# Three rounds per pair of heads in a forgetting attention, with moved work at the head of the program and at a scan

## The reference

```python
def diff_attention(q, k, v, lam, lam_init, sub_g):     # 4 heads of 2 x 64, causal, 128-query blocks
    s = einsum('bqhmd,bkhmd->bhmqk', qi, kf) * scale + bias
    p = softmax(s); attn = p[:, :, 0] - lam * p[:, :, 1]
    o = einsum('bhqk,bkhe->bqhe', attn, vf)

def fox_mixer(q, k, v, f_raw, f_bias, q_norm_w, k_norm_w):   # 16 heads of 64
    cum = cumsum(log_sigmoid(f_raw + f_bias))
    for start in range(0, s, 128):                     # query blocks 0..3, keys 0..end
        end = start + 128
        logits = qh[start:end] @ kh[:end].T * scale + cum[start:end, None] - cum[None, :end]
        p = softmax(where(causal, logits, -inf))
        outs.append(p @ vh[:end])

x = x + concat([y_ssd, y_fox]) @ w_out                 # 2048 x 1024
x = x + (silu(gate) * val) @ w_down                    # after rms_norm, w_up, causal conv of 3 taps
```

## Time and profile before

| | us |
|---|---|
| median of 3 runs | 1915.64 |
| lowest, highest | 1915.46, 1917.94 |
| the profiled execution, whole | 1915.37 |
| its span, first to last instruction | 1913.5 |
| PE busy in the span | 1886.8 |
| DVE busy | 1181.0 |
| ACT busy | 790.7 |
| POOL busy | 140.0 |

### The profile page before, as it was taken

The page is one execution under the profiler, slowest core; times in us unless marked ns, Lnnn a source line. Parts: engine busy times, 40 slices in busy tenths (PEclk is TensorE's granted clock), DMA queues, the critical chain, the costliest instruction groups (busy, mean ns, idle before and its releaser), DMA issues.

```text
span 1913.5 us, 24463 instructions
## 1 busy us (share of the span) xinstructions
PE 1886.8 (99%) x9034; PEld 1504.5 (79%) x9034; DVE 1181.0 (62%) x1831; ACT 790.7 (41%) x1200; POOL 140.0 (7%) x102
## 2 busy tenths in 40 slices
PE   7999999999999999999999999999999999999999
PEld 6767888888887788888888887877666688888887
DVE  5686677356646866763576498565656566744762
ACT  4355444133435654441244433432466543422431
POOL 1011100000021110000000101111201020000000
PEclk9999999999999999999999999999999999999999
DMA  5211322322231122223222322344433123223222
GB/s 214 67 62 49 99 99 73 119 94 97 73 107 65 45 89 89 88 88 110 97 92 83 113 88 99 135 165 143 161 105 110 34 88 110 77 99 110 88 77 99
DMA packets 38304, 186.51 MB, mean 97 GB/s; under 512 B 4384, under 2 KB 4768, under 8 KB 23376
## 3 DMA queue, kind: packets, MB, share of 16 engines
q1 hardware_dynamic: 37936, 185.22, 28.5%
q10 hardware_dynamic: 288, 0.23, 0.0%
HBM read 176.95 MB, written 8.49 MB: 97 GB/s over the span
## 4 chain that ended last, share of the span: by engine, by line
PE 91%; DVE 5%; ACT 2%; issue 1%; DMA 0%; SPq 0%; POOL 0%; ACTq 0%; DVEq 0%; POOLq 0%
PE banks L709 55%; PE banks L1181 21%; PE banks L759 4%; DVE w_lo L1851 1%; PE banks L1120 1%; PE banks L1098 1%; DVE w_lo L2100 1%; PE banks L1107 1%; PE banks L1254 1%; PE banks L1225 1%; DVE tmp L2233 1%; PE banks L1070 1%; ACT w_hi L1334 1%; PE banks L1237 1%; PE banks L1194 1%
## 5 line engine op out<-in xcount | busy, mean ns | idle before, releaser
L709 PE MATMUL banks<-xn_hi,w_hi 128*128 128x512 f32 x1240 | 486.9, 393 | 10.5 <-DVE w_lo L2606 6.9
L709 PE MATMUL banks<-xn_hi,w_lo 128*128 128x512 f32 x1240 | 483.4, 390 | 0.0
L709 PE MATMUL banks<-xn_lo,w_hi 128*128 128x512 f32 x1240 | 478.2, 390 | 0.0
L1334 ACT ACTIVATE w_hi<-raw 128x2048 fp32r<-128x2048 f32 (+2 forms) x134 | 228.3, 1704 | 227.9 <-PE banks L709 192.3
L1851 DVE TENSOR_TENSOR w_lo<-raw,w_hi 128x2048 fp32r<-128x2048 f32 (+2 forms) x134 | 275.8, 2058 | 46.1 <-ACT w_hi L1334 45.7
L709 PEld LDWEIGHTS banks<-xn_hi,w_hi 128*128 128x128 f32 x1240 | 233.5, 188 | 62.3 <-DMA con<-consts 5.9
L709 PEld LDWEIGHTS banks<-xn_lo,w_hi 128*128 128x128 f32 x1240 | 233.5, 188 | 49.5 <-issue 1.4
L709 PEld LDWEIGHTS banks<-xn_hi,w_lo 128*128 128x128 f32 x1240 | 233.5, 188 | 48.8
L1396 ACT ACTIVATE tmp<-scaled_h,par 128x512 f32<-128x512 f32 x132 | 100.8, 809 | 349.8 <-DVE scaled_h L1896 349.7
L1896 DVE TENSOR_TENSOR scaled_h<-banks,token_rs 128x512 f32<-128x512 f32 x132 | 85.0, 686 | 186.3 <-PE banks L709 166.0
L1181 PE MATMUL banks<-xn_hi,w_hi 128*128 128x512 f32 x408 | 165.3, 405 | 1.0 <-DVE big L1946 0.6
(11 more groups left out here) (270 smaller groups left out, 2578.3 us busy)
## 6 DMA issues: line engine op xcount, KB each, us to landing
raw<-weights SPq DMA_DIRECT2D x116, 1024.0 KB, 4.9
raw<-weights SPq DMA_DIRECT2D x24, 768.0 KB, 4.3
raw<-weights SPq DMA_DIRECT2D x24, 640.0 KB, 3.9
big<-scratch SPq DMA_DIRECT2D x40, 256.0 KB, 4.8
att<-scratch SPq DMA_DIRECT2D x16, 256.0 KB, 4.7
scratch<-stage SPq DMA_DIRECT2D x12, 256.0 KB, 4.4
scratch<-con SPq DMA_DIRECT2D x12, 256.0 KB, 2.0
out<-x SPq DMA_DIRECT2D x4, 512.0 KB, 4.0
```

Of the source, the lines that this page charges most:

```text
L709: return pe.matmul(psum[:, 2 * p + m, :], w[:, at_:at_ + P], x_part(k), start=start, stop=stop)
L1334: act.activation(w_hi[:, sl], raw[:, sl], ACT.Identity).then_inc(hi_done, 1)
```

## The change

1. **Forgetting attention:** three rounds per pair in place of four. Blocks 0 and 1 share a round, side by side in the bank (columns 0 to 127 and 128 to 383), then block 2, then block 3. 26 steps in place of 34, with 12 products in each of 22 steps and 6 in each of the last four. ACT copies a pair's values at the first step of that pair, where it did so in the last step of the pair before. `x_scaled` stands ahead of the halves of `w_lo`, behind the bank reads.
2. **Scan:** products of steps 0 to 9 are 18, 20, 4, 4 and six times 3, in place of 18, 14 and eight times 4. `columns_taken` moves into `xbc`, between the taps of the last two chunks.
3. **Differential attention:** `w_lo` of the output slabs is made in two halves, in two successive steps.
4. **Head:** ACT rounds slab 1 behind the first square, and slab 2 ahead of `token_norm`; DVE subtracts slab 2 ahead of the first bank reads.

```diff
-S_PREP, S_POST, X_STEPS = 15, 4, 32
-S_FILL = weave([("S_Z", 4), ("X_IN", 12)], [18, 14] + [4] * 8 + [8] * 5 + shares(568, 2 * SSD_HEADS) + [24] * S_POST)
-X_FILL = weave([("S_OUT", 4), ("X_OUT", 2)], shares(192, 19) + shares(96, 15))
+S_PREP, S_POST = 15, 4
+X_ROUNDS = [(0, 1), (2,), (3,)]
+X_STEPS = 8 * len(X_ROUNDS)
+S_FILL = weave([("S_Z", 4), ("X_IN", 12)], [18, 20] + [4, 4] + [3] * 6 + [8] * 5 + shares(568, 2 * SSD_HEADS) + [24] * S_POST)
+X_FILL = weave([("S_OUT", 4), ("X_OUT", 2)], [12] * 22 + [6] * 4)
...
+        def f_blocks(r):
+
+            out, col = [], 0
+            for i in X_ROUNDS[r % 3]:
+                out.append((i, col, (i + 1) * P))
+                col += (i + 1) * P
+            return out
...
+                def mask(r):
+
+                    if r:
+                        pe.wait_ge(f_max, f_done(r))
                     for m in range(2):
+                        for i, col, w in f_blocks(r):
+                            pe.matmul(psum[:, 4 + m, col + i * P:col + (i + 1) * P], ident_b[:, :], mask_b[:, :],
+                                      start=(col == 0), stop=False, skip_group_check=True)
...
                     if it + 1 < X_PAIRS:
-                        if g % 4 < 2:
-                            x_norm_job(2 * (it + 1) + g % 4)
-                        elif g % 4 == 2:
+                        if g % 3 < 2:
+                            x_norm_job(2 * (it + 1) + g % 3)
+                        else:
                             x_turn_v(it + 1)
...
                 o = FIRST["A_OUT"]
+                hi(2, 0)
                 token_norm()
-                hi(2, 0)
                 hi(3, 0)
...
                 for g in range(X_STEPS + 2):
-                    it = g // 4
-                    if g % 4 == 2 and it >= 1:
+                    it = g // 3
+                    if g % 3 == 0 and 1 <= it < X_PAIRS:
+                        x_v_copy(it)
+                    if g % 3 == 2 and it >= 1:
                         high(it - 1)
...
             for c in range(DC):
-                if c == 3:
+                if c == 1:
                     hi_piece(1, 0, 2, hi_half)
                     hi_piece(1, 1, 2)
...
+                lo(2, 0)
                 dve.wait_ge(rs_ready, 1)
                 evacuated(0, 0)
-                lo(2, 0)
...
-                    if g:
-                        for s in A_FILL[1][g - 1]:
-                            lo_piece(s + 1, 0, 1)
+                    for q in range(2):
+                        if g > q:
+                            for s in A_FILL[1][g - q - 1]:
+                                if s + 1 >= o:
+                                    lo_piece(s + 1, q, 2)
+                                elif q == 0:
+                                    lo_piece(s + 1, 0, 1)
...
                         if m == 0:
                             lo(a + n + 2, 0)
+                            if n == NSLAB["S_XBC"] - 1:
+                                columns_taken()
...
                 for t in range(S_STEPS):
                     h, part = head_step(t)
-                    if t == 0:
-                        columns_taken()
...
+                    if g % 3 and it + 1 < X_PAIRS:
+                        x_scaled(2 * (it + 1) + g % 3 - 1)
                     for q in range(2):
                         if g >= q + 1:
                             for s in X_FILL[1][g - q - 1]:
                                 lo_piece(s + 1, q, 2)
-                    if g % 4 in (1, 2) and it + 1 < X_PAIRS:
-                        x_scaled(2 * (it + 1) + g % 4 - 1)
```

More of the change, by code:

```diff
@@ new lines, in scores @@
+                def scores(r):
+                    it = r // 3
+                    if r % 3 == 0:
+                        pe.wait_ge(f_qk, 2 * it + 2)
+                    for i, col, w in f_blocks(r):
+                        for m in range(2):
+                            h = 64 * m
+                            last = pe.matmul(psum[:, 4 + m, col:col + w], f_qn[it % 2][h:h + 64, i * P:(i + 1) * P], f_kn[it % 2][h:h + 64, 0:w],
+                                             start=False, stop=True, skip_group_check=True)
+                            if i == X_ROUNDS[r % 3][-1]:
+                                last.then_inc(f_scored, 1)
@@ L1108, in turn, with values @@
+                def turn(r):
+                    for m in range(2):
+                        pe.wait_ge(f_fin, 2 * r + m + 1)
+                        if r:
+                            pe.wait_ge(f_copied, 2 * r - 1 + m)
+                        for j in range(f_width(r) // P):
+                            last = pe.transpose(psum[:, 6 + m, j * P:(j + 1) * P], f_prob(m, r)[:, j * P:(j + 1) * P], ident)
                         last.then_inc(f_pt, 1)
-                def values(g):
-                    it, i = g // 4, g % 4
-                    if i == 0:
+                def values(r):
+                    it = r // 3
+                    if r % 3 == 0:
@@ L1756, in copy @@
-                def copy(g):
-                    w = f_width(g)
+                        for i, col, w in f_blocks(r):
+                            n += 1
+                            act.wait_ge(f_max, n)
+                            pr = f_prob(m, r)[:, col:col + w]
+                            act.activation(pr, pr, ACT.Exp, scale=-1.0, bias=neg_max[:, 2 * i + m:2 * i + m + 1],
+                                           accum_out=row_sum[:, 2 * i + m:2 * i + m + 1]).then_inc(f_exp, 1)
+                def copy(r):
+                    w = f_width(r)
@@ L2254, in xbc, with columns_taken @@
                         running_sums()
+            def columns_taken():
+                dve.wait_ge(turned, 1)
+                dve.tensor_copy(tok[:, 0:384], psum[:, 4, 0:384]).then_inc(taken, 1)
             def in_turn(ins):
@@ L2322, in evacuate @@
                     dve.tensor_tensor(stage[v % 2], c_bank(u), token_rs[:, :], ALU.mult).then_inc(unit_read, 1)
-                def columns_taken():
-                    dve.wait_ge(turned, 1)
-                    dve.tensor_copy(tok[:, 0:384], psum[:, 4, 0:384]).then_inc(taken, 1)
                 def ends_taken():
@@ L2511, in maxima @@
                     for m in range(2):
[L2512 to L2521 removed]
+                        dve.wait_ge(f_scored, 2 * r + m + 1)
@@ new lines, in maxima, with finish @@
+                        for i, col, w in f_blocks(r):
+                            dve.tensor_tensor_reduce(
+                                out=f_prob(m, r)[:, col:col + w], in0=psum[:, 4 + m, col:col + w], in1=f_bias[it % 2][m][:, 0:w], scale=-1.0,
+                                scalar=3e38, op0=ALU.add, op1=ALU.min, accum_out=neg_max[:, 2 * i + m:2 * i + m + 1]).then_inc(f_max, 1)
+                def finish(r):
+                    blocks = f_blocks(r)
+                    n0, n1 = 2 * blocks[0][0], 2 * blocks[-1][0] + 2
+                    dve.wait_ge(f_exp, f_done(r + 1))
+                    me.mark(dve.reciprocal(row_inv[:, n0:n1], row_sum[:, n0:n1]))
@@ L2522, in finish @@
                     me.wait()
                     for m in range(2):
-                        pr = f_prob(m, g)[:, 0:w]
-                        dve.tensor_scalar(pr, pr, row_inv[:, n + m:n + m + 1], None, ALU.mult).then_inc(f_fin, 1)
+                        for i, col, w in blocks:
+                            pr = f_prob(m, r)[:, col:col + w]
+                            last = dve.tensor_scalar(pr, pr, row_inv[:, 2 * i + m:2 * i + m + 1], None, ALU.mult)
+                        last.then_inc(f_fin, 1)
```

109 lines of the change are left out of this document (38 added, 71 removed).

## The result

The changed kernel takes **1901.74 us** (median of 4, 1901.62 to 1901.86) against 1916.79 for the kernel before measured with it (1915.46 to 1918.68): a ratio of 0.9925, 95% interval 0.9913 to 0.9938. The forecast was 1904.5, range 1900.5 to 1910.0. Direction and range held; the gain was 15 us where 11 had been forecast. Beside a median stands the ratio to the kernel before as measured in the same job, whose own median went from 1915.6 to 1916.8; one of e2's eleven executions took 6703.42 us, for no reason on record, and is outside its ratio. The span of the profiled execution went from 1913.5 to 1900.0 us, 13.5 less.

A forecast was written before the change was run, and what follows sets the result against it. TensorE, busy 1886.8 of 1913.5 us, was taken as the bound. Gains of 4.6 + 0.7 + 1.4 + 2.6 + 1.6 = 10.9 us off the profiled 1915.37 gave 1904.5 us, range 1900.5 to 1910.

The forecast's parts named there:

- Head: Start of the kernel: first wait 2.2, clock 1.65 and slab 2's wait 0.75 give 4.6 us gain, bounds 2.2 to 5.3.
- The first wait: Head, TensorE's 2.95 us wait before slab 1: TensorE starts at 20.5 instead of 22.70, 2.2 us gain, bounds 1.5 to 2.9.
- The clock: Head, behind the wait for slab 1: TensorE's clock stays up instead of 0.53, 1.65 us gain, bounds 0 to 1.65.
- the sum that needs them ... covers that: Head: squares end later, about 22.2, but their sum stands behind slab 1's first 24 products, some 6 us after its start.
- Differential attention: Halving DVE's 3.13 us subtraction frees 1.5 us, but the next finish ends only 0.7 us earlier: 0.7 us gain, bounds 0 to 1.5.
- Start of the scan: The 3.0 us wait goes, new waits of 0.9 and 0.7 us come: 1.4 us gain, bounds 0.7 to 3.2.
- Seams: Forgetting attention: 0.32 us per round beyond its products, eight rounds fewer: 2.6 us gain, bounds 2.2 to 3.2.
- Waits of forgetting attention: Of 3.6 us of TensorE's waits with refills, 2.0 stay: 1.6 us gain, bounds -2 (a loss) to 3.6.
- (a): Rival, head: the clock falls all the same or slab 1 stays late, 3 us less gain, 1907.5 us; chance 0.10.
- (b): Rival, forgetting attention: seams given back, one us more wait in each of five pairs, 1909.5 us; chance 0.12.
- (c): Rival, forgetting attention: TensorE waits for scaled keys at seven pairs; at 3 us a pair, 1925.5 us; chance 0.03.
- (d): Rival, whole kernel: each wait moves to the next join and the gain misses the end, 1913 us; chance 0.05.

The follow-up runs named there:

- e2: Kernel before with only the head changed (slab 1 rounded behind the first square, slab 2 ahead of norm and bank reads): 1912.48 us, ratio 0.9978.
- e5: Kernel before with one more wait on POOL, whose sums of squares start only when all eight squares are there: 1913.73 us, ratio 0.9985.
- e10: Changed kernel with ACT's rounding of slab 1 put back behind the third square: 1905.55 us.
- e1: Kernel before with only forgetting attention changed (three rounds per pair, new quotas, keys scaled ahead of the halves): 1908.89 us, ratio 0.9958.
- e4: Kernel before with only the differential attention's subtraction of slabs 8 to 10 cut into halves in two steps: 1915.65 us, ratio 0.9997.
- e8: Kernel before, still four rounds per pair, with forgetting attention's 288 woven products spread evenly over 34 steps: 1917.69 us, ratio 1.0006.
- e6: Changed kernel with forgetting attention's products in proportion again, 13 or 14 in the first 14 steps, 8 in the last 12: 1901.05 us.
- e11: Changed kernel with 16 more semaphore increments, on order 0's score products in each joined round, that nobody waits for: 1901.78 us.
- e12: Changed kernel with proportional forgetting-attention quotas, two more products in differential-attention steps 11 and 12, slab 107's halves behind the scan's last copies: 1899.85 us, ratio 0.9919.
- e7: Changed kernel with DVE's scaling of the next pair's keys put back behind the slab halves in forgetting attention: 1909.86 us, ratio 0.9969.

## Why the prediction was right, and where it was off

- **What bounds the kernel.** Right: nearly all was gained in TensorE's waits and seams, and behind forgetting attention the lengths agree to 0.1 us.
- **Head, 4.6 forecast, 4.6 measured** from the first matmul on; the mechanism held, and that the figure was hit is luck, since errors cancel and the head by itself varies by about 1 us from trace to trace. The first wait lost 2.9 us, not 2.2. Of the 0.7 more, 0.5 is that TensorE itself came 0.5 us later to slab 1 in the changed kernel's trace; it began slab 1 at 20.34 us, where 20.5 had been forecast. The step that failed was the second half's duration, which I put between alone and contended (1.7 us, until 20.4): it took 1.22, though POOL worked beside it for its last 0.8 us, and in the other kernels with this head TensorE began slab 1 at 19.7 to 20.2. So the reading by which the second half pays while POOL runs, near 1.8 us for the wait, did not come true: POOL began after the half had begun. The clock gave 1.5 for 1.65, slab 2 0.9 for 0.75. And "the sum that needs them ... covers that" was wrong by 0.6 us: the statistic behind slab 1's first half now waits, since contention moved onto the sums of squares (4.10 us). Slab 0, which no edit touches, took 0.16 us more. e5 and e10 carry the reason.
- **Differential attention, 0.7 forecast, 0.1 measured.** The row shows one wait of 1.8 us become two of 0.7 and 0.5. The step that failed is "ends then only some 0.7 us earlier": all of it was given back, which was the lower bound. The first half took 2.06 us, not 1.2 to 1.6: it began inside an addition of POOL with 0.98 us left. The 3.13 us of before were themselves 0.84 us longer than the 2.29 that 2048 columns take alone, for the same cause, and the halves did not remove it. The first half, POOL's addition, then the two waits:
```profile
132.65 2.06 DVE L2122 TENSOR_TENSOR w_lo<-raw,w_hi 128x1024 fp32r<-128x1024 f32 x1
...
132.15 1.48 POOL L657 TENSOR_TENSOR tn<-big 128x512 f32<-128x512 f32 x1 [4.80 <-DVE big L2025]
...
136.59 0.55 PE L887 MATMUL banks<-con,att 128*128 128x128 f32 x3 [0.73 <-DVE att L2020]
...
141.19 0.66 PE L887 MATMUL banks<-con,att 128*128 128x128 f32 x4 [0.50 <-DVE att L2020]
```
- **Start of the scan, 1.4 forecast, 1.35 measured,** with the two new waits at the places and in the sizes named (0.9 and 0.7). Timelines of DVE and TensorE after, against the earlier trace rows:
```profile
1162.51 1.69 DVE L2122 TENSOR_TENSOR w_lo<-raw,w_hi 128x1024 fp32r<-128x1024 f32 x1
...
1162.74 0.63 PE L977 MATMUL banks<-con,big 128*128 128x128 f32 x4 [0.70 <-DVE att L2364]
1164.94 0.63 PE L977 MATMUL banks<-con,big 128*128 128x128 f32 x4 [0.88 <-DVE att L2364]
```
- **Seams, 2.6 forecast, 4.4 measured.** The mechanism was right, the size was outside its bounds (2.2 to 3.2): per round it was 0.32 and is 0.55. The step that failed is reading seams off the timeline's merged rows: they show the product's 0.10 and the mask's 0.10, of the value group 0.12 of 0.15, and nothing of the 0.20 at the score group, since the whole group is one row. The four score records of 128 columns there take 0.42 us from their start to the first product's, and cost 0.22 inside a joined group.
- **Waits of forgetting attention, 1.6 forecast, 3.5 measured,** near the better bound. With the seams the stage lost 7.9 us where the terms had 4.2 (the forecast's list of signs says 4.6): that is more than the 2.6 us by which the whole profiled gain exceeds the forecast, and the range held with 1.2 us to spare. Of 2.0 us that I left standing only 0.7 listed ones stand, near the last pair, where they had been placed. Timeline of TensorE after, which shows a joined round, against the earlier trace rows:
```profile
1393.65 0.82 PE L1124 MATMUL banks<-con,big 128*128 128x128 f32 x6
1394.30 0.39 PE L1103 MATMUL banks<-mask_b,ident_b 128*128 128x128 bf16 x4
1394.53 0.61 PE L1091 MATMUL banks<-con,big 128*128 128x128 f32 x4
1395.06 0.88 PE L1138 MATMUL banks<-big 128*64 128x128 f32 x12
1395.87 0.93 PE L1113 MATMUL banks<-big 64*128 64x128 f32 x8
1396.73 0.50 PE L1199 MATMUL banks<-mix_hi,w_hi 128*128 128x512 f32 x1
```
- **The sum.** The profiled executions differ by 13.5 us where 10.9 was forecast: +1.8 of seams, +1.9 of waits, less 0.6 in differential attention and 0.4 of the later start. The medians differ by 15: that of before had risen to 1916.8, 1.4 above its profiled execution. e2 and e5 show one possible cause, the clock behind the scan's 3 us wait, which costs 1.6 us in their profiled executions and nothing in those of before, e1, e4 and e8. Whether that was so in the other executions of before isn't shown, but their spread fits: 1913.0 to 1919.0 in all jobs, while the kernels without a long wait in head or scan stayed within 0.9 us each (changed, e6, e11, e12).
- **Rivals.** (a) did not happen in the change, and e10 is what it looks like: 3.8 us. (b) did not happen. (c), slower by keys that come too late, is a real mechanism: e7 has it at four of seven pairs, 7.6 us. It was right that the scaling ahead of the round's own halves keeps it away; the forecast had not seen that this edit carries the whole gain of the rounds. (d) did not happen, except for the halves in differential attention.

## What to carry to other kernels

Before two engines' times are added up, look whether an instruction of one starts inside an instruction of the other; here what had looked like slow subtractions was a hold that one moved start took away. Where kinds of matmul alternate, price each entry and exit from single start times and not from merged rows, and join groups before tuning the order within them. A small operation that another engine waits for belongs ahead of any operation that can be held; here, without that single move, the joining was worth almost nothing. Work that can wait goes where its engine is idle (e12), while more cover on one wait helps only if the engine behind it is not late for the stage as a whole.

## What the runs showed of the hardware

- The same idle stretch of 3.05 us cost 1.6 us of clock behind it in e2 and e5 and nothing in before, e1, e4 and e8, at the same place of the program. At the head, waits of 2.5 to 3.5 us had a window at 0.51 to 0.63 behind them each time. What decides is open.
- DVE's 128 x 1024 subtraction takes 1.22 us alone. Begun inside an addition of POOL, it takes longer by what is left of that addition, less 0.14 us (2.31 with 1.23 left, 2.06 with 0.98 left); begun before POOL's, it takes 1.22 still. DVE's 128 x 512 addition goes from 0.69 to 1.6 us in the same way (with 1.05 left).
- Behind a wait of up to 0.4 us for slab 1 the clock stayed at 1.00 in all seven kernels with the changed head, and in e5 behind 0.18.
- A score product that increments a semaphore costs no more than one that doesn't (e11). Entering a group of score products costs 0.1 us and leaving it 0.1 us; a mask before value products costs 0.09 us more than before another mask or the norm's matmul.
